# First weight panel in one transfer, and the bias look-up moved behind its first four chunks: a two-block transformer on one core

## What is computed

```python
def first_block(x, attn_norm_g, w_in, ...):
    h = rmsnorm(x, attn_norm_g[l])
    z = h @ w_in[l]                       # z[..., :256] is u, the first thing computed
    y_a = gmlp_mixer(z[..., :o_a], ...)
    y_c = diff_attn_mixer(..., rel_bias, l)
...
# in the attention
bias = rel_bias[t5_causal_bucket(rel)].astype(jnp.float32)
s = s + bias.transpose(2, 0, 1)[None, :, None]
```

## Time and profile before

| what | value |
|---|---|
| median of 3 runs | 1496.45 us (1495.83 to 1496.84) |
| the profiled execution | 1496.79 us |
| span of its trace | 1495.1 us (1.69 us less) |
| TensorE busy | 1485.2 us, 99% |
| ACT, DVE busy | 564.9 us (38%), 875.8 us (59%) |
| mean DMA rate | 100 GB/s; 230 in the first fortieth |

### The profile page before, as it was taken

One profiled execution on the slowest core, in us unless ns is written; L12 is line 12 of the kernel. 1 busy time (PEld: TensorE's weight loads), 2 busy tenths in 40 slices (PEclk: granted clock), 3 DMA queues, 4 the chain that ended last, 5 costly groups with the idle time before them and its releaser, 6 DMA issues.

```text
span 1495.1 us, 20331 instructions
## 1 busy us (share of the span) xinstructions
PE 1485.2 (99%) x7240; PEld 1226.0 (82%) x7240; DVE 875.8 (59%) x1425; ACT 564.9 (38%) x836; POOL 23.9 (2%) x21
## 2 busy tenths in 40 slices
PE   9999999999999999999999999999999999999998
PEld 7878888888888888888888887888888888888887
DVE  6737764675665555443468877965665653255433
ACT  5215553333433333333325646444443331123231
POOL 0000000000000000000000000000000000000000
PEclk9999999999999999999999999999999999999999
DMA  6623222223322332333333223322222322233321
GB/s 230 231 85 99 77 90 85 86 81 103 110 89 96 98 98 98 99 102 110 113 99 104 94 98 102 110 76 84 63 79 85 109 90 96 98 99 98 99 71 57
DMA packets 44445, 149.17 MB, mean 100 GB/s; under 512 B 4792, under 2 KB 7352, under 8 KB 44260
## 3 DMA queue, kind: packets, MB, share of 16 engines
q1 hardware_dynamic: 39840, 138.43, 28.3%
q10 hardware_dynamic: 4548, 9.96, 1.9%
HBM read 146.24 MB, written 6.06 MB: 102 GB/s over the span
## 4 chain that ended last, share of the span: by engine, by line
PE 98%; DMA 0%; issue 0%; DVE 0%; ACT 0%; SPq 0%; POOLq 0%; POOL 0%; DVEq 0%
PE ps L1168 31%; PE ps L1170 31%; PE ps L1169 31%; PE ps L1319 1%; PE ps L1332 1%; PE ps L2338 1%; PE ps L1209 0%; DMA x<-x_dram 0%; PE ps L2438 0%; PE ps L1202 0%; PE ps L2358 0%; PE ps L1377 0%; PE ps L2370 0%; PE ps L2283 0%; PE ps L1274 0%
## 5 line engine op out<-in xcount | busy, mean ns | idle before, releaser
L528 ACT ACTIVATE wh<-stage 128x1024 fp32r<-128x1024 f32 x254 | 268.9, 1059 | 545.7 <-PE ps L1170 541.3
L1168 PE MATMUL ps<-hh,wh 128*128 128x512 f32 x1088 | 430.7, 396 | 0.8 <-DVE hl L775 0.5
L1170 PE MATMUL ps<-hh,wl 128*128 128x512 f32 x1088 | 424.3, 390 | 0.0
L1169 PE MATMUL ps<-hl,wh 128*128 128x512 f32 x1088 | 423.6, 389 | 0.0
L764 DVE TENSOR_TENSOR wl<-stage,wh 128x1024 fp32r<-128x1024 f32 x253 | 309.2, 1223 | 185.2 <-ACT wh L528 184.6
L1168 PEld LDWEIGHTS ps<-hh,wh 128*128 128x128 f32 x1088 | 204.3, 188 | 47.5 <-issue 4.1
L1170 PEld LDWEIGHTS ps<-hh,wl 128*128 128x128 f32 x1088 | 204.2, 188 | 43.6
L1169 PEld LDWEIGHTS ps<-hl,wh 128*128 128x128 f32 x1088 | 204.5, 188 | 39.6
L1168 PE MATMUL ps<-ah,wh 128*128 128x512 f32 (+1 forms) x448 | 171.7, 383 | 0.0
L1170 PE MATMUL ps<-ah,wl 128*128 128x512 f32 (+1 forms) x448 | 171.5, 383 | 0.0
L1169 PE MATMUL ps<-al,wh 128*128 128x512 f32 (+1 forms) x448 | 171.5, 383 | 0.0
(11 more groups left out here) (340 smaller groups left out, 1838.1 us busy)
## 6 DMA issues: line engine op xcount, KB each, us to landing
stage<-stream_dram SPq DMA_DIRECT2D x254, 512.0 KB, 3.3
bias_lines<-bias_line ACTq DMA_DIRECT2D x1, 3840.0 KB
bias<-bias_lines ACTq DMA_DIRECT2D x4, 512.0 KB, 4.8
x<-x_dram SPq DMA_DIRECT2D x3, 512.0 KB, 7.7
out_dram<-x SPq DMA_DIRECT2D x12, 128.0 KB, 1.8
bias<-bias_lines ACTq DMA_DIRECT2D x4, 256.0 KB, 3.1
mem<-mem_dram ACTq DMA_DIRECT2D x1, 1024.0 KB, 4.9
stage<-stream_dram SPq DMA_DIRECT2D x2, 256.0 KB, 4.1
```

Of the source, the lines that this page charges most:

```text
L528: A(parts_of(b, p)[0], b.stage[:, p.slot, :], ACT.Copy).then_inc(s.hi_ready, 1)
L1168: MM(out, wh, xh, start=start, stop=False, skip_group_check=True)
L1169: MM(out, wh, xl, start=False, stop=False, skip_group_check=True)
L1170: return MM(out, wl, xh, start=False, stop=stop, skip_group_check=True)
```

## The change

Panel 0 comes in one transfer; ACT waits for it once and still rounds it in two pieces, so that DVE can follow piece by piece. The look-up's two transfers are issued behind panel 1 (x's second transfer and panel 1 now come ahead of them). On TensorE the look-up's product is placed behind chunks 0 to 3 of panel 0 and ahead of those of panel 1. The last product of zeros is 512 instead of 256 columns wide and waits for x's first transfer instead of for its first rounded chunk. One semaphore is dropped and one renamed.

```diff
@@ sync_program
-    half = D // 2
-    sp.dma_start(b.stage[:, 0, 0:half], stream[0, :, 0:half]).then_inc(s.first_in, 16)
-    sp.dma_start(b.stage[:, 0, half:D], stream[0, :, half:D]).then_inc(s.load[0], 16)
-    sp.dma_start(b.onehot[0:NB, :], dram["onehot"]).then_inc(s.line_in, 16)
-    sp.dma_start(b.tables[0:NB, :], dram["tables"]).then_inc(s.line_in, 16)
+    sp.dma_start(b.stage[:, 0, :], stream[0]).then_inc(s.load[0], 16)
     for c in range(1, 4):
         sp.dma_start(b.x[:, 2 * c:2 * c + 2, :], dram["x"][:, 2 * c:2 * c + 2, :]).then_inc(s.x_in[c], 16)
         if c == 1:
             sp.dma_start(b.stage[:, 1, :], stream[1]).then_inc(s.load[1], 16)
+            sp.dma_start(b.onehot[0:NB, :], dram["onehot"]).then_inc(s.line_in, 16)
+            sp.dma_start(b.tables[0:NB, :], dram["tables"]).then_inc(s.line_in, 16)
@@ scalar_program
-    act.wait_ge(s.first_in, 16)
+    act.wait_ge(s.load[0], 16)
     A(b.wh[:, 0, 0:half], b.stage[:, 0, 0:half], ACT.Copy).then_inc(s.first_hi, 1)
-    act.wait_ge(s.load[0], 16)
     A(b.wh[:, 0, half:D], b.stage[:, 0, half:D], ACT.Copy).then_inc(s.hi_ready, 1)
@@ tensor_program
     for n in range(3):
         blank(T)
-    pe.wait_ge(s.line_in, 32)
-    MM(b.ps[0:HEADS, 4, :], b.tables[0:NB, :], b.onehot[0:NB, :], start=True, stop=True).then_inc(s.line_done, 1)
-    pe.wait_ge(s.x_hi, 1)
-    blank(M)
+    pe.wait_ge(s.x_in[0], 16)
+    blank(T)
     for part in (range(0, 4), range(4, KT)):
         for u in range(2):
             p = Panel(P_U + u)
...
             if k == KT - 1:
                 ins.then_inc(s.panel_done, 1)
+            elif u == 0:
+                pe.wait_ge(s.line_in, 32)
+                MM(b.ps[0:HEADS, 4, :], b.tables[0:NB, :], b.onehot[0:NB, :], start=True,
+                   stop=True).then_inc(s.line_done, 1)
```

More of the change, by code:

```diff
@@ L219, in semaphores @@
         "acted2 act2_hi act2_ready final_scaled")
-    s.gate_in = nc.alloc_semaphore("gate_in")
-    s.first_in, s.first_hi = named("first_in first_hi")
+    s.small_in = nc.alloc_semaphore("small_in")
+    s.first_hi = nc.alloc_semaphore("first_hi")
     (s.mem_scaled, s.silued, s.blank_set) = named(
@@ L1543, in block2_scalar @@
     for r in range(2):
-        act.dma_start(b.wgu[64 * r:64 * r + 64, :], dram["wgu"]).then_inc(s.gate_in, 16)
+        act.dma_start(b.wgu[64 * r:64 * r + 64, :], dram["wgu"]).then_inc(s.small_in, 16)
     act.dma_start(b.masks[:], dram["late"].rearrange("p (l q) -> p l q", q=P)).then_inc(s.late_in, 16)
@@ L2267, in logits @@
     def logits():
-        pe.wait_ge(s.gate_in, 32)
+        pe.wait_ge(s.small_in, 32)
         pe.wait_ge(s.evac, E_GLR + 1)
```

## The result

| | before | after |
|---|---|---|
| median, 20 runs each | 1496.63 us | 1498.24 us |
| lowest to highest | 1495.83 to 1497.67 us | 1497.65 to 1500.02 us |
| profiled execution, its span | 1496.79 us, 1495.1 us | 1497.83 us, 1496.1 us |
| ratio of the times | | 1.0013, 95% interval 1.0007 to 1.0019 |

The changed kernel is slower by about 1.6 us, less than 0.2%. The interval of the ratio excludes no change, and the median lies above the upper end of the range. Two things want an explanation. And the executions of after scatter over 2.4 us, with nine of the twenty spans at 1496.8 us or more. Before is not free of that: three of its twenty (1497.55 to 1497.67 us) lie 0.6 us above the other seventeen.

A forecast was written before the change was run, and what follows sets the result against it. TensorE's work bounds the kernel, so panel 1's start sets the end. A 0.26 us gain from x against a 0.43 us loss to the product gave +0.17 us: 1496.45 + 0.17 = 1496.62 us, range 1495.5 to 1497.9 us.

The forecast's parts named there:

- What bounds the kernel: TensorE's own work: from 12.45 us it runs nearly without a gap, so moving that start moves the end equally.
- Panel 0 in one transfer: Panel 0's load on SP's queue: lands at 5.6 us (5.2 to 6.9 us), costing nothing by itself.
- its bad case: Panel 0 landing at 6.9 us: x's third chunk would wait for DVE, 0.8 us lost.
- x is there by 6.4 us: x's first transfer on ACT's queue: landed by 6.4 us, before ACT starts its first x chunk at 6.68 us.
- its lower bound for x's second: Gain of x's second transfer at least 0, if x's first transfer beside it sets the rate.
- x's second transfer: Issued ahead of the look-up's transfers on SP: lands at 8.5 us, 0.26 us gained (bounds 0 and 1.4 us).
- The product's 0.43 us: Bias product on TensorE before panel 1: takes 0.95 us, 0.52 us of it formerly idle, so 0.43 us lost.
- The fallen clock: Rival: TensorE idles after the wider blank and loses its high clock for 5 us; 2.5 us, 1499.0 us; chance 0.04.
- The late panel rival: x lands as before or panel 0 late, delaying DVE's third chunk; +0.43 to +1.25 us, 1496.9 to 1497.7 us; chance 0.25.

The follow-up runs named there:

- tables_between: The changed kernel with the look-up's tables transfer (1.5 KB) moved up right behind panel 0 on SP's queue; 1496.25 us, -0.29 against before.
- filled: The changed kernel with four instead of three early products of zeros and a narrow one after the first rounded x chunk; 1498.07 us, +1.53 against before.
- product_moved: The kernel before with only the bias product moved behind panel 0's first four chunks; 1496.58 us, +0.44 against before.
- after_again: The changed kernel run once more as it is, nothing changed; 1497.69 us, +1.55 against before.
- after_halves: The changed kernel with panel 0 in two halves again, each waited for by itself; 1496.39 us, +0.25 against before.
- idle_only: The kernel product_moved without the narrow product of zeros and its wait; 1496.95 us, +0.41 against before.
- whole_panel: The kernel before with panel 0 in one transfer and nothing else; 1495.67 us, -0.47 against before.
- x_first: The changed kernel with ACT's two issues swapped, x's first transfer ahead of the gains; 1497.83 us, +1.16 against before.

## Why the prediction was wrong

- **What bounds the kernel**: right. Every run's span is panel 1's start plus 1482.6 to 1482.9 us.
- **Panel 0 in one transfer**: 5.6 us forecast, with a lower end of 5.2 us; 4.8 us measured. The sign was right and the size too small. This part alone gave 0.5 and 0.7 us in its two runs, where I had counted it at nothing, with a loss as its bad case.
- **"x is there by 6.4 us"**: this is the step that failed. I took the landing of x's first transfer from the rows of before and left it standing, while the change put 512 KB on SP's queue 0.01 us ahead of its issue. It landed at 7.8 us; TensorE's first real matmul went from 8.31 us to 9.57 us, not to 8.6 us. In tables_between SP issues x's second transfer and panel 1 0.47 us later; there x's first lands 1.8 us earlier than in filled, and the time is 1.8 us less (1496.25 against 1498.07 us). In after the two transfers of x moved side by side, packet for packet, from 4.4 to 6.4 us. The prediction had them beside each other too (its lower bound for x's second rests on that), but asked only what x's first does to x's second, not the reverse.
- **x's second transfer**: 8.5 us forecast, 7.1 us measured: 1.7 us earlier than in before's trace, beyond the end of my bounds (all of the earlier issue, 1.4 us). I asked what was ahead of it and not whom it would be ahead of. The gain I looked for was there, and it was taken from the transfer that ACT needed first.
- **The product's 0.43 us**: right for the schedule it was reckoned for. The product takes 0.95 or 0.96 us in every trace of a kernel that moves it (12.50 to 13.45 us in after), and product_moved, which isolates it, cost 0.44 us. (Of the 0.95 us, 0.52 us would have been idle, not 0.48 us as the prediction says in one place; its sum uses 0.52.) In after itself only 0.17 us of idleness stood there, between the twelfth matmul's end and panel 1's low part, so that 0.8 us of the product shows in its trace. The tables were in time (2.83 + 6.7 = 9.5 us).
- **The fallen clock**: held at a chance of 0.04, since two pauses of 0.5 us had been harmless. In after eight of twenty executions, and in after_again three of eleven, are 0.9 us or more longer than the shortest. In the one trace that shows the fall its price is smaller than I had priced it (1.6 us for a stretch of 3.4 us, not 2.5 us for one of 5); if the other long executions have the same cause, which their mean clock allows and does not prove, its frequency is far larger. The reason against it, "only 1.1 us of idleness are added", was built on the same failed landing: in after TensorE idles 0.71 us by the row and then 0.68 us before 9.57 us, in after_again 1.11 and 0.68 us. With x's first in time (tables_between, after_halves) TensorE idles 0.3 us there, and none of those 22 executions is long. idle_only, which has no last product of zeros at all, has long ones with every transfer in time.
- **The late panel rival** has the span's +1.0 us in its range (+0.43 to +1.25 us) and not the median's 1.6 us, and has it for a delay on DVE that didn't occur; DVE was done with panel 0 at 6.8 us.

So of the 1.6 us the product's place is 0.44 us by the run that isolates it, and up to 0.8 us once x's second transfer no longer holds the third chunk back. The late transfer is about 1.8 us against the same order of work with it in time; what the whole panel gives, and the earlier second transfer, are set against that. The clock lifts the mean further: filled against after_again hardly moves the median (+1.53 and +1.55 us on two chips), but has no long execution.

What stays open: why a transfer issued 0.46 us behind one on the other queue moves hardly at all until that one is nearly through, while one issued 0.01 us apart takes turns with it. A tie won by ACT's queue was not tried, nor a gap between 0.01 and 0.44 us. Open too is what makes an execution long. The clock is seen to fall in one trace; that idleness brings it rests on 6 long executions of 22 in after_again and idle_only against none of 11 in filled; and before, which idles little in its start, has 6 in 99.

## What to carry to other kernels

When a transfer is moved up, list what it now overtakes on every queue, the other engine's queue too, and ask which of these is wanted first: a landing read from the old trace is not a constant. Put the transfer that starts the chain ahead of large ones on the other queue by a clear gap; here a move of 1.5 KB did it. A small transfer is not safe for being small: if it has as many rows as the large one beside it, the two end together. And before a filler product is taken off an idle engine, look at what its idleness does to the clock over many executions: one profile may show either level.

## What the runs showed of the hardware

- Two transfers issued within 0.01 us on SP's and ACT's queues took turns packet by packet (88 and 88 packets in 1 us in whole_panel, 117 and 106 in 2 us in after). With rows of 728 bytes beside rows of 4 KB the counts stayed near each other (144 and 132 in x_first), so 91 KB landed with the 512 KB beside it.
- x's first transfer, on ACT's queue, landed at 7.8 to 8.1 us when it was issued 0.01 us behind x's second (512 KB) on SP's; issued 0.44 us or more ahead of that, at 5.8 to 6.7 us (1.8 us apart on one chip). In tables_between, from 4.4 to 5.2 us, the one ahead had the engines alone.
- A panel of 512 KB landed 0.8 us earlier in one transfer (4.95 us) than the second of two halves (5.76 us) on the same chip.
- The granted clock fell to 0.50 for 3.4 us in the midst of dense matmuls, after idle stretches of 1.11 and 0.68 us with 1.1 us of work between them; eight of the eleven executions of that program were at least 1.0 us shorter than each of the three longest. With a single idle stretch of 1.2 us in its trace, idle_only had long executions in 3 of 11, their clock not seen.
- The first six products of zeros took 4.46 us in one trace and 5.49 us in another of the same kernel.
